# A float32 decoder layer on one core: dense stages in another order, two sets of operand halves, down rows side by side

## What is computed

```python
z = rms_norm(x) @ w_in            # five column blocks: pool, lru_x, gelu, gate_a, gate_b
y_a = pool_mixer(u_pool) @ w_pool_proj          # windowed means (2, 4, 8, 16), a product per group, a scale
xr  = causal_depthwise_conv(u_lru, width 4)
r, i = sigmoid(per-head product of xr + bias)   # two of them
h_t = a_t * h_(t-1) + sqrt(1 - a_t^2) * i * xr,  a = exp(8 * r * log_sigmoid(lambda))
y_b = (h * gelu(u_gelu)) @ w_lru_proj
x  += (sigmoid(gate_a) * y_a + sigmoid(gate_b) * y_b) @ w_mix_out
q = rms_norm(x) @ w_q;  k, v = rms_norm(mem) @ w_kv
x  += softmax(q k^T / 16) v @ w_o               # 4 heads of 256
x  += top-4-of-32 experts: (clamped SwiGLU(xn @ w_gate_up + b)) @ w_down + b
out = rms_norm(x)
```

## Time and profile before

| what | value |
|---|---|
| time, three runs | 1359.19, 1355.86, 1358.99 us, median 1358.99 |
| profiled execution | 1357.88 us, span of the trace 1356.1 us |
| mean granted clock of TensorE | 0.981 |
| TensorE busy | 1220.3 us, 90% of the span |
| VectorE, ScalarE, GpSimd busy | 34%, 19%, 18% |
| HBM read | 459.74 MB, 340 GB/s over the span |

### The profile page before, as it was taken

How to read it: one execution, slowest core, us unless ns; L and a number is a source line. 1 busy time by engine, 2 the same in 40 slices (tenths; PEclk the granted TensorE clock), 3 DMA queues, 4 the chain that set the end, 5 groups by cost and what they waited for, 6 DMA issues and landing times.

```text
span 1356.1 us, 19336 instructions
## 1 busy us (share of the span) xinstructions
PE 1220.3 (90%) x7545; PEld 614.0 (45%) x7545; DVE 456.4 (34%) x701; ACT 251.1 (19%) x350; POOL 239.9 (18%) x73
## 2 busy tenths in 40 slices
PE   6996989989959999998999999989999999899996
PEld 6895988968733333332222233322222332222232
DVE  4848491223243323232222222322222223222223
ACT  6433643353330000000000000000000000000001
POOL 5784478766120000000000000000000000000000
PEclk9998999999968999999999999999999999999999
DMA  9541535441768999999999999999999999999993
GB/s 370 209 156 62 217 125 187 167 175 63 276 255 360 418 416 417 417 418 419 419 418 418 417 416 417 419 418 418 418 419 416 417 417 419 419 419 418 418 416 126
DMA packets 80544, 461.28 MB, mean 340 GB/s; under 512 B 7280, under 2 KB 7296, under 8 KB 41216
## 3 DMA queue, kind: packets, MB, share of 16 engines
q1 hardware_dynamic: 80016, 459.83, 84.0%
q0 software_dynamic: 208, 0.54, 0.1%
q10 hardware_dynamic: 288, 0.45, 0.1%
HBM read 459.74 MB, written 1.05 MB: 340 GB/s over the span
## 4 chain that ended last, share of the span: by engine, by line
PE 42%; DMA 37%; SPq 10%; DVE 6%; ACT 2%; issue 2%; POOL 0%; DVEq 0%; ACTq 0%; POOLq 0%
DMA late<-in_w_gate_up 37%; PE ps L1157 17%; SPq L299 6%; PE ps L1044 4%; PE ps L1046 4%; PE ps L1045 4%; SPq L304 4%; DVE s L725 2%; PE ps L1208 2%; PE ps L1182 2%; PE ps L1078 2%; PE ps L1062 2%; PE ps L1064 2%; PE ps L1063 2%; PE ps L1216 1%
## 5 line engine op out<-in xcount | busy, mean ns | idle before, releaser
L1157 PE MATMUL ps<-late,s 128*64 128x512 f32 x992 | 474.1, 604 | 64.1 <-DMA late<-in_w_gate_up 59.0
L1158 PE MATMUL ps<-late,s 128*64 128x512 f32 x992 | 474.0, 604 | 0.0
L1157 PEld LDWEIGHTS ps<-late,s 128*64 128x64 f32 x992 | 117.9, 136 | 387.2 <-DMA late<-in_w_gate_up 218.4
L359 POOL TENSOR_TENSOR wlo<-raw,whi 128x2048 fp32r<-128x2048 f32 x47 | 227.0, 4839 | 131.5 <-ACT whi L438 131.5
L1157 PE MATMUL ps<-raw,s 128*64 128x512 f32 x408 | 187.3, 602 | 1.0 <-DVE s L891 1.0
L1158 PE MATMUL ps<-raw,s 128*64 128x512 f32 x408 | 187.3, 602 | 0.0
L1044 PE MATMUL ps<-act_hi,whi 128*128 128x256 f32 x576 | 165.9, 288 | 13.6 <-issue 4.8
L940 DVE TENSOR_TENSOR res<-res,ps 128x1024 f32<-128x1024 f32 x66 | 80.6, 1221 | 269.7 <-PE ps L1208 269.6
L1046 PE MATMUL ps<-act_hi,wlo 128*128 128x256 f32 x576 | 164.4, 285 | 0.0
L1045 PE MATMUL ps<-act_lo,whi 128*128 128x256 f32 x576 | 164.3, 285 | 0.0
L589 ACT ACTIVATE s<-ps 128x512 f32<-128x512 f32 x64 | 34.7, 594 | 591.5 <-PE ps L1158 591.5
(11 more groups left out here) (174 smaller groups left out, 1099.4 us busy)
## 6 DMA issues: line engine op xcount, KB each, us to landing
late<-in_w_gate_up SPq DMA_DIRECT2D x248, 1024.0 KB, 20.6
raw<-in_w_down SPq DMA_DIRECT2D x96, 1024.0 KB, 25.9
raw<-in_dense SPq DMA_DIRECT2D x51, 1024.0 KB, 4.8
s<-in_w_down SPq DMA_DIRECT2D x32, 1024.0 KB, 21.8
raw<-in_w_gate_up SPq DMA_DIRECT2D x6, 1024.0 KB, 5.9
s<-in_w_gate_up SPq DMA_DIRECT2D x2, 1024.0 KB, 4.8
s<-in_mem SPq DMA_DIRECT2D x2, 512.0 KB, 5.3
res<-in_x SPq DMA_DIRECT2D x1, 1024.0 KB, 12.1
```

What stands on the lines that cost most here:

```text
L359: nc.gpsimd.tensor_tensor(wlo[:, m % SPL, :], raw[:, n % RAW, :], whi[:, m % SPL, :].bitcast(F32), ALU.subtract)\
L1157: nc.tensor.matmul(ps[0:SLOTS, bank, :], x_tile, lower, start=start, stop=stop)
L1158: return nc.tensor.matmul(ps[SLOTS:P, bank, :], x_tile, upper, start=start, stop=stop)
```

## The change

The dense part gets another order, with the same products in it:

- `DENSE` and TensorE's list: transposes of x, `lrux`, `pool`, `gelu`, then the per-head stages `ra`, `rx`, `grp`, then `ga`, `gb`, `pp`, `lp`, transposes of mem, `mix`, `ka` (half of the keys), transposes of x1, `kb` (the other half), `q`, scores, `v`, transposes of the probabilities, their products with v, `o`.
- There are two sets of `act_hi` and `act_lo`, and the table `SET` says which operand has which. For them `raw` has four slots instead of six. `whi` and `wlo` stay at three each, and `FIRST` and `LATE` are drawn up anew over the 16 slots: two halves of a set now belong to `FIRST`.
- x is loaded first, in two pieces with a semaphore for each; mem is loaded behind the second chunk of `lp`, behind a wait for the scan.
- The argument of GeLU is made ahead of the scale of `grp`; the copies of the banks of `v` and of the turned probabilities are shared by ScalarE and VectorE; halves are made per tile pair behind the merge.
- `w_down` is laid out anew on the host, so that the two rows of a partition lie side by side; a down transfer reads 128 rows of 8 KB for 256 of 4 KB, the same bytes.

```diff
-RAW = 6
+RAW = 4
...
-for _name, _n in (("k", 4), ("v", 4), ("lrux", 4), ("pool", 4), ("ra", 1), ("rx", 1), ("grp", 1), ("gelu", 4),
-                  ("ga", 4), ("gb", 4), ("pp", 4), ("lp", 4), ("mix", 4), ("q", 4), ("o", 4)):
+for _name, _n in (("lrux", 4), ("pool", 4), ("gelu", 4), ("ra", 1), ("rx", 1), ("grp", 1), ("ga", 4), ("gb", 4),
+                  ("pp", 4), ("lp", 4), ("mix", 4), ("ka", 2), ("kb", 2), ("q", 4), ("v", 4), ("o", 4)):
...
+SET = {"h": 0, "pool": 1, "lru": 0, "merged": 1, "mem": 0, "xn": 1, "attn": 1}
...
+S1, S5, SPLIT, SETS = RAW, RAW + 1, RAW + 2, RAW + 2 + 2 * SPL
+SLOTS_W = SETS + 4
+FIRST = [SETS, SETS + 1, 0, 1, S1, S5, 2, 3]
+LATE = [SPLIT + i for i in range(2 * SPL)] + [SETS + 2, SETS + 3]
...
-                if n == 1:
-                    sp.dma_start(res[:], x.rearrange("(t p) d -> p t d", p=P)).then_inc(S["in_x"], 16)
+                if n == DENSE["lp"] + 1:
+
+                    sp.wait_ge(S["scan_done"], KT)
+                    for t in range(TT):
+                        sp.dma_start(mem_rows[:, t, :], mem[t * P:(t + 1) * P, :]).then_inc(in_mem[t], 16)
...
-                rows2 = w_down[bass.ds((i * 2 + half) * D + j * 2 * P, 2 * P), :]
-                sp.dma_start(slots[at].rearrange("p (f d) -> p f d", d=D),
-                             rows2.rearrange("(f p) d -> p f d", p=P)).then_inc(loaded[at], 16)
+                sp.dma_start(slots[at], w_down[bass.ds((i * 2 + half) * (D // 2) + j * P, P), :])\
+                    .then_inc(loaded[at], 16)
...
+            for j in range(4):
+                evacuate("gelu", j, lambda j, b: nc.scalar.activation(
+                    gelu_f[:, 2 * j:2 * j + 2, :], two(b), ACT.Copy).then_inc(S["freed_act"], 1))
+                weights_after("gelu", j)
...
-            act.wait_ge(S["scan_done"], KT)
-            for j in range(4):
                 evacuate("ga", j, lambda j, b: nc.scalar.activation(
                     siga_f[:, 2 * j:2 * j + 2, :], two(b), ACT.Sigmoid).then_inc(S["freed_act"], 1))
                 weights_after("ga", j)
+                if j == 0:
+
+                    act.wait_ge(S["inner_done"], 1)
+                    nc.scalar.activation(b_f, b_f, ACT.Sqrt, scale=-1.0).then_inc(S["mult_done"], 1)
...
+                high_of(pool_f, "pool", j)
+            act.wait_ge(S["scan_done"], KT)
+            for j in range(4):
                 evacuate("gb", j, lambda j, b: nc.scalar.activation(
...
             for j in range(4):
                 low_of(pool_f, "pool", j)
-
-            dve.wait_ge(S["freed_act"], evacuated(UNIT["gb"] + 3)[1])
+            for j in range(4):
+                low_of(hs_f, "lru", j)
...
-            transposed("memT", mem_rows, 0)
-            feature_major("k", "mem")
-            token_major("v", "mem")
-            transposed("xT", xs_rows, 1)
-            feature_major("lrux", "h")
-            feature_major("pool", "h")
+            transposed("xT", xs_rows, 0)
+            for name in ("lrux", "pool", "gelu"):
+                feature_major(name, "h")
             pe.wait_ge(S["xr_done"], KT)
             per_head("ra", xr_f)
             per_head("rx", xr_f)
             pe.wait_ge(S["pool_done"], 1)
             per_head("grp", pool_f)
-            for name in ("gelu", "ga", "gb"):
-                feature_major(name, "h")
+            feature_major("ga", "h")
+            feature_major("gb", "h")
             feature_major("pp", "pool")
             feature_major("lp", "lru")
+            transposed("memT", mem_rows, 1)
             token_major("mix", "merged")
+            feature_major("ka", "mem", 2)
             transposed("x1T", xn_rows, 2)
+            feature_major("kb", "mem", 2)
             feature_major("q", "xn")
...
-              "w_down": one("w_down").reshape(EXPERTS * D, D),
+              "w_down": by_rows(one("w_down").reshape(EXPERTS * D, D)).reshape(-1, CHUNK),
```

More of the change, by code:

```diff
@@ L207, in build @@
         slots = [raw[:, i, :] for i in range(RAW)] + [s1[:, 0:CHUNK], s5[:, 0:CHUNK]] \
-            + [late[:, i, :] for i in range(GU_CHUNKS)]
+            + [late[:, i, :] for i in range(SLOTS_W - SPLIT)]
         x32, h32 = (s6[:, i * BANK:(i + 1) * BANK].rearrange("p (k c) -> p k c", c=SLOTS) for i in range(2))
@@ L256, in build @@
         S = {n: sem(n) for n in names}
+        in_x = [sem(f"in_x{t}") for t in range(TT)]
         in_mem = [sem(f"in_mem{t}") for t in range(TT)]
@@ L750, in _ @@
             dve.sem_inc(S["pool_done"], 1)
+            dve.wait_ge(S["freed_act"], evacuated(UNIT["gelu"] + 3)[1])
+            link(V.tensor_tensor(gtmp_f, gelu_f, gelu_f, ALU.mult))
+            link(V.tensor_scalar(gtmp_f, gtmp_f, 0.044715, 1.0, ALU.mult, ALU.add))
+            V.tensor_tensor(gtmp_f, gtmp_f, gelu_f, ALU.mult).then_inc(S["gelu_arg"], 1)
             def scaled(j, b):
@@ L782, in _ @@
                 low_of(pool_f, "pool", j)
-            dve.wait_ge(S["freed_act"], evacuated(UNIT["gb"] + 3)[1])
+            for j in range(4):
+                low_of(hs_f, "lru", j)
+            dve.wait_ge(S["freed_act"], evacuated(UNIT["ga"] + 3)[1])
             units("pp", 4, lambda j, b: V.tensor_tensor(
@@ L787, in _ @@
                 .then_inc(S["freed_dve"], 1))
-            for j in range(4):
-                low_of(hs_f, "lru", j)
+            normalise(1, mem_rows, mem_rows)
             def merge(j, b):
@@ L797, in merge @@
                     .then_inc(S["m_done"], 1)
-            units("lp", 4, merge)
+            dve.wait_ge(S["freed_act"], evacuated(UNIT["gb"] + 3)[1])
             for j in range(4):
-                low_of(m_f, "merged", j)
+                evacuate("lp", j, merge)
+                if j:
+                    low_of(m_f, "merged", j - 1)
+            low_of(m_f, "merged", 3)
+            low_from_psum("memT", "mem", "norm_mem")
             def onto_residual(j, b):
@@ L1031, in tiles_ready, with feature_major @@
                 pe.wait_ge(S["lo_done"], split_tiles(operand, k))
-            def feature_major(name, operand):
-                for j in range(KT // 2):
+            def feature_major(name, operand, n_chunks=KT // 2):
+                hi, lo = act_hi[operand], act_lo[operand]
+                for j in range(n_chunks):
                     w_hi, w_lo = (w.rearrange("p (k n) -> p k n", n=2 * P) for w in parts(name, j))
@@ L1109, in _ @@
                 last.then_inc(S["unit_done"], 1)
+            token_major("v", "mem")
             for h in range(HEADS):
@@ L1118, in _ @@
             for h in range(HEADS):
-                pe.wait_ge(S["freed_act"], evacuated(UNIT["pT"] + h)[1])
+                for made in (UNIT["v"] + h // 2, UNIT["v"] + 2 + h // 2, UNIT["pT"] + h):
+                    eng, count = evacuated(made)
+                    pe.wait_ge(freed[eng], count)
                 b = begin(UNIT["oT"] + h)
```

178 lines of the change are left out of this document (85 added, 93 removed).

## The result

| | before | changed |
|---|---|---|
| median of four runs | 1358.49 us | 1335.26 us |
| span of the profiled execution | 1356.1 us | 1333.8 us |
| start of the unbroken stream of pieces | 424.17 us | 408.29 us |
| last gate-and-up landing | 1321.46 us | 1297.69 us |
| from there to the end | 34.6 us | 36.1 us |

The ratio is 0.9846, 95% interval 0.9804 to 0.9887. By the medians the changed kernel is faster by 23 us, and the prediction of 1340.8 stood 5.5 us too high. The ratio is that of the means: three of the four executions took 1334.2 to 1335.7 us and one 1343.5, which pulls it up and widens its interval.

What follows compares the result with a forecast made beforehand. TensorE's dense part was taken to bound the stream's start and DMA transfers its pace. A dense part 10.4 us shorter plus 7.8 from down rows gave 18.2 off 1357.9, 1339.7, plus 1.1 for the median: 1340.8 us; range 1329 to 1354.

Steps and rivals of the forecast that it cites:

- The two limits: Whole kernel: TensorE's dense part sets the weight stream's start, DMA transfers its pace; end is start plus pieces plus tail.
- Convolution covered: Dense part: three stages on h keep TensorE busy until VectorE's convolution ends, so 12.0 us of waiting go.
- A new wait in its place: Per-head stages: ga's weight copies, waiting for slots, delay ScalarE; TensorE idle 1.8 us in rx and 8.8 before grp.
- The scan later: Scans end at 158; gb's last weight copy behind ScalarE's wait for them leaves TensorE 4.9 us idle.
- The wait at pp: Start of pp: four low halves stand behind GpSimd's pieces on VectorE, leaving TensorE 6 us idle.
- The lower clock: Dense part: three 3.3 us stretches at half clock behind the long waits, 5.0 us lost, 1.5 less than before.
- Behind pp: Stages after pp: other stages cover the hand-overs; all earlier waits go but some 0.6 us.
- Down rows: Expert weight stream: 8 KB rows bring down transfers to gate-and-up pace, 116 pieces at 0.067 us, 7.8 us saved.
- Rows without effect: Rival on down transfers: 8 KB rows bring nothing, 1348.6 us; chance 0.12.
- That the new waits eat the gain: Rival on the dense part: new waits cost another 10.4 us, leaving it as long as before, 1351 us; chance 0.12.
- That the new waits are shorter: Rival on the waits at gb's last chunk and pp: up to 10.9 us more gained, 1330 us; chance 0.12.
- GpSimd as the bound: Rival on ga to q: GpSimd's weight pieces fall 0.8 us behind per chunk, 22 us in all, 1363 us; chance 0.04.

Runs made afterwards that it cites:

- the two runs: Kernel before with 8 KB down rows alone: 1349.67 us; changed kernel with the old 4 KB down rows: 1342.78 us.
- two of the experiments: Changed kernel with x1's transposes right behind mix, then keys, q and v: 1351.02 us; changed kernel with GeLU's stage behind the per-head stages: 1352.90 us.
- the last kernel: Changed kernel with ga's copies, root and pool halves moved, ScalarE waiting on the first scan, GpSimd's pieces halved, pp's weight copies ahead of ScalarE's LRU wait: 1318.69 us.

## Why the prediction was right, and where its size was off

- **The two limits** and what they make of a gain held: 15.9 us of earlier start arrived at the end in full. The start was forecast near 413 and came at 408.29.
- **Convolution covered.** Forecast to end near 82 with TensorE at 86; it ended at 82.1. Right.
- **A new wait in its place.** 1.8 and 8.8 us forecast, 2.2 and 9.1 measured, ended by ScalarE as said. That the copies cause it is shown by the run that moved them: both waits went.
- **The scan later.** 158 forecast, 158.1 measured. The wait for gb's last chunk, 4.9 forecast and 4.98 measured, agrees in part by luck: TensorE came to it at 162.3 and not at 160, and it ended at 167.2 and not at 165. It came later because grp began 1.2 us later than booked and TensorE ran at the lower level behind that wait (0.50 until 117), and the wait ended later because GpSimd's piece behind the scan took 6.5 us, in turn with VectorE's products, and not the 4.6 booked.
- **The wait at pp** is the term that was mis-sized: 6 us forecast, 1.2 measured. The low halves were late, as I had said; all four were forecast for 176.7, the third ended at 177.7. But I had TensorE at pp at 170.8, and it came at 175.0: 2.2 us later because gb's last chunk began later, 2.0 because it ran at the lower level behind that wait. I had booked the lower clock as a term of its own (5.0) and let TensorE reach pp without it. A wait for work that does not depend on TensorE ends at a fixed time, so what TensorE loses ahead of it is taken off the wait. And I had TensorE wait for all four low halves, where it can begin with the first: it worked 1.6 us on the first two. 6 - 4.2 - 1.6 + 1.0 is the 1.2 measured. The two windows of lower clock around the long waits are:

```profile
107.00:117.00 10.00, 4.33 (x10) 3.50 (x11) 3.21 (x4) 8.51 (x17) 4.50 (x1) 0.50 0.07 31
164.00:171.50 7.50, 4.26 (x20) 4.29 (x21) 7.50 (x2) 1.13 (x1) 7.50 (x2) 0.55 0.38 140
```

- **The lower clock.** Three stretches of it were forecast, behind the waits of 8.8, 4.9 and 6. There were three, but behind 2.2, 9.1 and 4.98, and none behind pp: the number was right by luck.
- **Behind pp** no wait was left, where 0.6 was allowed for and 1.1 at the second chunk; 1.7 us better. With the 4.8 of pp and 0.5 less of TensorE's busy time, less 0.8 at the other waits, this is the 6.2 us by which the dense part was shorter than forecast: 330.30 - 313.75 = 16.6 for 10.4. Of the 6.2, 0.7 did not reach the start of the stream and 1.5 went in the tail; the spans differ by 22.3 for 18.2. The other 1.4 us of the 5.5 lie between the medians and the profiled executions.
- **Down rows.** 7.8 forecast, 7.9 in the trace, 7.5 in the two runs. The Trainium skill (DMA: Bandwidth & Descriptors, Specifications) has line rate from 512 bytes on; rows of 4 KB moved 408 to 409 GB/s here and rows of 8 KB 415 to 424, so the measurement speaks against the rule by 2% to 4%, and it decided.
- **The tail** cost 1.5 us that the sum did not have. It is no effect of the change: in the profiled runs here, none of which changes TensorE's work for the experts, the tail is 34.6 or some 36.2 us, by whether the clock falls in it: its mean granted clock is 0.93 or 0.94 in four runs with the short tail (the kernel before among them) and 0.88 to 0.90 in four with the long one (the changed kernel among them).
- **The rivals.** Rows without effect is refuted by two runs. That the new waits eat the gain was true in kind for 17 of the 32 us and not in size. That the new waits are shorter came true for the one at pp. GpSimd as the bound did not decide in the changed kernel. The mechanism behind it, turns with VectorE, was part of what kept 8 of 13 us back once the copies were moved (6.61 and 5.53 us for instructions of 2.29 and 1.23). How large a part is not shown: changes of ScalarE's and VectorE's order brought the 12 us from 1330.7 to 1318.7 but for the 1 to 2 us that halving GpSimd's pieces is worth.

## What to carry to other kernels

A copy or prefetch step that waits for a buffer is also a wait for all that stands behind it on its engine: put it where the buffer is sure to be free, not where the code is handy. The waits of 2.2 and 9.1 us in the changed kernel and those of 7.2 and 15.5 us in two of the experiments had such a copy ahead of them. The opposite happens too: the waits of 4.98 us were for copies that stood behind a wait of the same engine for another one. When you add up waits, carry one time through the whole chain: a wait for work on another engine and the losses ahead of it do not add, and a stage can begin with the first piece of its operand. And before you take a wait away, ask what it kept apart: here it kept GpSimd out of VectorE's scans, and without it the kernel was 7 us slower.

## What the runs showed of the hardware

- VectorE's operations on SBUF alone and GpSimd's take turns, one instruction of each. A product of 2048 elements took 2.29 us alone, 4.4 behind a half piece and 6.5 to 6.6 behind a whole one; eight scans took 9.06, 13.46, 17.69 and 26.59 us. One scan follows the next in 0.58 us where no piece lies between, eight in 4.7, and the four times are 4.7 and about 4.4 for each of one, two, three and five pieces. GpSimd's piece itself went from 4.6 to up to 6.5.
- Down transfers of the same bytes moved 2% to 4% more per second in four short windows with rows of 8 KB than with rows of 4 KB, with the DMA engines' share at 0.99 to 1.03; over the stream of 116 such pieces among the gate-and-up ones it was 7.9 us of 897.
- Shorter waits of TensorE kept its clock up as well. In the last kernel, with none over 1.2 us, the granted clock was 1.00 from 14.7 to 314 us. In the dense parts of the profiled kernels it was 0.50 behind each wait of 4 us and more (4.16 and 11.97 in the kernel before, 4.98 and 9.05 in the changed one); behind waits of 1.7 to 3.3 us it was in some places (2.2 in both) and in others not (1.69 and 1.88 in the kernel before, 3.30 with the copies later).
